# First gate blocks of an expert in front of the branch that picks its body, and shared by all bodies (Trainium2, one core)

## The reference, cut to what matters

```
def moe_swiglu(h, w_router, w_gu, w_down):
    logits = (h @ w_router).astype(jnp.float32)
    top_vals, top_idx = lax.top_k(logits, TOP_K)
    gates = jax.nn.softmax(top_vals, axis=-1)
    comb = ...
    for e in range(N_EXPERTS):
        y = y + comb[..., e:e + 1] * swiglu(h, w_gu[e], w_down[e])
```

## Time and profile before

| | us |
|---|---|
| median of 3 runs | 1783.42 (1782.84 to 1784.57) |
| the profiled execution | 1783.2 |
| its span, first to last instruction | 1781.4 |
| mean granted clock of TensorE, share of full | 0.962 |
| from the first gate matmul of expert 0 to the last of the program | 648 to 1771 |

### The profile page before, as it was taken

How to read it: one execution, slowest core, us unless ns; L and a number is a source line. 1 busy time by engine, 2 the same in 40 slices (tenths; PEclk the granted TensorE clock), 3 DMA queues, 4 the chain that set the end, 5 groups by cost and what they waited for, 6 DMA issues and landing times.

```text
span 1781.4 us, 20893 instructions
## 1 busy us (share of the span) xinstructions
PE 1637.2 (92%) x7345; PEld 1330.9 (75%) x7346; DVE 1267.4 (71%) x1092; ACT 1021.9 (57%) x872; POOL 10.6 (1%) x26
## 2 busy tenths in 40 slices
PE   7999999999899869999999999899999599898996
PEld 5887778888787657777778878778887477677775
DVE  6745554444588569999988888555554599799796
ACT  4344343443456537878867767544443488687684
POOL 0000000000000000000000000000000000000000
PEclk9999999999999869999999999899999799899998
DMA  9653455555522129999999889656564399899894
GB/s 355 194 189 109 163 177 189 188 188 189 188 97 71 47 76 377 397 365 387 394 345 370 329 322 364 237 185 212 192 217 156 126 382 395 296 386 395 302 394 177
DMA packets 191592, 450.84 MB, mean 253 GB/s; under 512 B 8492, under 2 KB 8892, under 8 KB 191420
## 3 DMA queue, kind: packets, MB, share of 16 engines
q1 hardware_dynamic: 189212, 445.35, 69.8%
q10 hardware_dynamic: 2336, 4.85, 0.7%
HBM read 449.13 MB, written 1.05 MB: 253 GB/s over the span
## 4 chain that ended last, share of the span: by engine, by line
PE 71%; DVE 11%; DMA 8%; ACT 5%; issue 4%; DVEq 0%; SPq 0%; ACTq 0%; POOL 0%; POOLq 0%
PE bank L1140 19%; PE bank L1141 19%; PE bank L1144 19%; DMA raw<-in_moe_w_down 8%; DVE wlo L691 6%; PE bank L1147 4%; ACT whi L396 4%; PE bank L1148 3%; DVE y L929 2%; PE bank L1417 1%; PE bank L1418 1%; PE bank L1315 1%; PE bank L1317 1%; PE bank L1433 1%; PE bank L1434 1%
## 5 line engine op out<-in xcount | busy, mean ns | idle before, releaser
L691 DVE TENSOR_TENSOR wlo<-raw,whi 128x2048 fp32r<-128x2048 f32 x422 | 962.6, 2290 | 323.1 <-ACT whi L396 322.2
L396 ACT ACTIVATE whi<-raw 128x2048 fp32r<-128x2048 f32 x422 | 804.9, 1915 | 457.6 <-PE bank L1144 376.9
L1140 PE MATMUL bank<-whi,xx 128*128 128x512 f32 x1184 | 481.3, 406 | 62.7 <-issue 28.1
L1141 PE MATMUL bank<-wlo,xx 128*128 128x512 f32 x1184 | 473.2, 400 | 0.0
L1144 PE MATMUL bank<-whi,xx 128*128 128x512 f32 x1184 | 473.0, 400 | 0.0
L1140 PEld LDWEIGHTS bank<-whi,xx 128*128 128x128 f32 x1184 | 230.2, 194 | 114.5 <-issue 35.9
L1144 PEld LDWEIGHTS bank<-whi,xx 128*128 128x128 f32 x1184 | 229.3, 194 | 49.8
L1141 PEld LDWEIGHTS bank<-wlo,xx 128*128 128x128 f32 x1184 | 230.2, 194 | 46.7
L1147 PE MATMUL bank<-whi,hT 128*128 128x512 f32 x336 | 138.8, 413 | 23.7 <-DVE wlo L691 22.5
L1147 PE MATMUL bank<-whi,xx 128*128 128x512 f32 x336 | 133.3, 397 | 0.2 <-DVE wlo L691 0.2
L1148 PE MATMUL bank<-wlo,hT 128*128 128x512 f32 x336 | 132.3, 394 | 0.0
(11 more groups left out here) (200 smaller groups left out, 1246.0 us busy)
## 6 DMA issues: line engine op xcount, KB each, us to landing
raw<-in_moe_w_gu SPq DMA_DIRECT2D x224, 1024.0 KB, 7.6
raw<-in_moe_w_down SPq DMA_DIRECT2D x112, 1024.0 KB, 7.8
raw<-in_ffn_w_gu SPq DMA_DIRECT2D x28, 1024.0 KB, 5.1
raw<-in_ret_w_in SPq DMA_DIRECT2D x24, 1024.0 KB, 6.6
raw<-in_ffn_w_down SPq DMA_DIRECT2D x14, 1024.0 KB, 4.8
raw<-in_conv_w_pw SPq DMA_DIRECT2D x12, 1024.0 KB, 5.1
raw<-in_ret_w_out SPq DMA_DIRECT2D x8, 1024.0 KB, 4.9
res<-in_x SPq DMA_DIRECT2D x2, 512.0 KB, 4.9
```

What stands on the lines that cost most here:

```text
L396: nc.scalar.activation(whi[base % SPLIT][:, :], raw[base % RAW][:, :], ACT.Copy).then_inc(hi_done, 1)
L691: nc.vector.tensor_tensor(wlo[base % SPLIT][:, :], raw[base % RAW][:, :], whi[base % SPLIT][:, :].bitcast(f32), ALU.subtract).then_inc(lo_ ...
L1140: nc.tensor.matmul(dst, ah, bh, start=start, stop=False)
L1141: last = nc.tensor.matmul(dst, ah, bl, start=False, stop=stop and al is None)
```

## The change

TensorE: tile 0's two gate blocks leave the bodies and are issued once, behind the load of `need` and in front of the branches (`gates_first(0, ...)`), without raising `pe_done`. The bodies stand in the order light to wide. A body begins with `nothing`, a matmul of 4 columns that adds zeros to bank 0; in a narrow body it raises `pe_done` by 2. In a wide body the order is now: `nothing`, gather of tile 1, wait for `yl_done`, scatter, wait for the new semaphore `xel2_done`, tile 1's gate blocks, which raise `pe_done` by 2. ScalarE: `hi` of block 1 is in front of `xh_gathered2`. VectorE: the low part of tile 1 is behind `lo` of block 1 and `y_lo`, and raises `xel2_done`.

```diff
@@ ScalarE, expert @@
                 xh_gathered(e)
+                hi(B_MOE + 1, six)
                 if tiles == 2:
                     xh_gathered2(wide_before(act, e))
-                hi(B_MOE + 1, six)
                 y_hi(B_MOE + 6 * six)
@@ VectorE, expert @@
-                xl_gathered(e, tiles, n2)
+                xl_gathered(e)
                 lo(B_MOE + 1, six)
                 y_lo(e)
+                if tiles == 2:
+                    xl_gathered2(n2)
                 lo(B_MOE + 2, six)
@@ TensorE @@
+            def nothing(dst):
+                return nc.tensor.matmul(dst[:, 0:4], zeros[:, 0:P], zeros[:, 0:4], start=False, stop=True)
...
+            def gates_first(tile, six):
+                for half in range(2):
+                    pe.wait_ge(lo_done, B_MOE + half + 1 + 6 * six)
+                    slot_ = (B_MOE + half) % SPLIT
+                    for c in range(4):
+                        kc = 4 * half + c
+                        last = product(bank[tile][:, :], xh[:, kc, tile, :], xl[:, kc, tile, :],
+                                       whi[slot_][:, c * BANK:(c + 1) * BANK], wlo[slot_][:, c * BANK:(c + 1) * BANK],
+                                       kc == 0, tile == 1 and kc == DC - 1)
+                return last
+
             def expert(e, kinds):
                 six, done, tiles = STEPS * e, STEPS * e + STEPS, len(kinds)
                 gates = (FULL,) * tiles
                 n2 = wide_before(pe, e) if tiles == 2 else None
+                gates_end = nothing(bank[0])
                 if tiles == 2:
                     gather(e, 1).then_inc(gather2_ps, 1)
-                pe.wait_ge(xel_done, e + 1)
-                columns(B_MOE, bank[0:2], 0, kinds=gates, six=six)
-                columns(B_MOE + 1, bank[0:2], 1, kinds=gates, six=six)
-                pe.wait_ge(yl_done, e + 1)
-                scatter(0, SCAT).then_inc(scat_ps, 1)
+                    pe.wait_ge(yl_done, e + 1)
+                    scatter(0, SCAT).then_inc(scat_ps, 1)
+                    pe.wait_ge(xel2_done, n2 + 1)
+                    gates_first(1, six).then_inc(pe_done, 2)
+                else:
+                    gates_end.then_inc(pe_done, 2)
+                    pe.wait_ge(yl_done, e + 1)
+                    scatter(0, SCAT).then_inc(scat_ps, 1)
                 pe.wait_ge(hTl_done, done)
@@ TensorE, loop over the experts @@
                 need = need_of(pe, e)
-                with pe.If(need > 1):
-                    with pe.If(need > 2):
-                        expert(e, (FULL, FULL))
-                    with pe.Else():
-                        expert(e, (FULL, HALF_FULL))
+                pe.wait_ge(xel_done, e + 1)
+                gates_first(0, STEPS * e)
+                with pe.If(need < 1):
+                    expert(e, (HALF_FULL,))
                 with pe.Else():
-                    with pe.If(need > 0):
+                    with pe.If(need < 2):
                         expert(e, (FULL,))
                     with pe.Else():
-                        expert(e, (HALF_FULL,))
+                        with pe.If(need < 3):
+                            expert(e, (FULL, HALF_FULL))
+                        with pe.Else():
+                            expert(e, (FULL, FULL))
```

More of the change, by code:

```diff
@@ L237, in trunk @@
         xel_done = sem("xel_done")
+        xel2_done = sem("xel2_done")
         ohT_ps = sem("ohT_ps")
@@ L1048, in _, with xl_gathered @@
             own(last)
-            def xl_gathered(e, tiles, n):
+            def xl_gathered(e):
                 for q in range(2):
@@ L1054, in xl_gathered, with xl_gathered2 @@
                                                    xh[:, 4 * q:4 * q + 4, 0, :].bitcast(f32), ALU.subtract)
[L1055 to L1060, removed]
-                last.then_inc(xel_done, 1)
+                last.then_inc(xel_done, 1)
+            def xl_gathered2(n):
+                dve.wait_ge(xeh2_done, n + 1)
+                for q in range(2):
+                    last = nc.vector.tensor_tensor(xl[:, 4 * q:4 * q + 4, 1, :],
+                                                   bank[2 + q][:, :].rearrange("p (c n) -> p c n", c=4),
+                                                   xh[:, 4 * q:4 * q + 4, 1, :].bitcast(f32), ALU.subtract)
+                last.then_inc(xel2_done, 1)
             def y_lo(e):
```

## The result

The changed kernel takes 1769.78 us (median, 1765.62 to 1771.41), the kernel before 1783.13 beside it: a ratio of 0.992 with a 95% interval of 0.9904 to 0.9937, so 0.8% faster. The forecast was 1769.2. The profiled execution took 1770.99 us, of which the span is 1769.2; the span before was 1781.4, so the trace has to account for 12.2 us.

The account below looks back on a forecast made before the run. TensorE, busy 92% of the span, was taken to stand idle at expert starts waiting for its own code. Terms -2.5 + 6.6 + 5.6 - 6.1 - 11.0 - 6.6 = -14.0 took 1783.2 to 1769.2 us; own range 1765 to 1773.

Parts of the forecast that it names:

- (a): Start of expert 0: first gate block starts 4.0 earlier, second finds its split done; -2.5 us, between -4 and 0.
- (b): First use of the loop's end in page 22: expert 1 now begins with a stall; +6.6 us, between 0 and 8.2.
- (c): Later weight-slot release delays ScalarE's block 3 split: +1.4 us per HALF_FULL expert, +5.6 for experts 1, 5, 6 and 7.
- nothing makes it up: HALF_FULL steps: VectorE, 14.68 busy of 15.12, bounds them, so the late release's 1.4 us per expert stays.
- (d): Start of wide expert 4: gates fill the 3.89 idle, scatter then waits 3.4 for yl; -6.1 us, between -9 and 0.
- (e): Start of expert 5: one stall of 3.8 to 5.3, first gates at 1390.7 instead of 1401.67; -11.0 us.
- (f): Starts of experts 6 and 7: five pages in use instead of seven, one of two stalls gone; -6.6 us.
- R1: Rival: both later stalls, at experts 6 and 7, go since five pages are few; 1761 us, chance 0.24.
- R3: Rival: far loop end, page 22, fetched anew at every boundary, starts of 1, 2, 3 stall; 1797.5 us, chance 0.08.
- R4: Rival: stalls belong to the loop's way back alone, not the branch into a body; +7.9, 1791 us, chance 0.07.
- R2: Rival: both later stalls stay, since the wide body pushes out page 14; 1776 us, chance 0.15.
- R5: Rival: late release costs its upper bound, +5.2, and the wide start brings half; 1777 us, chance 0.08.

Follow-up runs that it names:

- experiment 4: Changed kernel with ScalarE's y_hi put ahead of the second gathered tile's evacuation in the wide body alone: 1764.27 us, ratio 0.9897.
- experiment 2: Kernel before with only TensorE's four bodies reordered light to wide, first gates left in each body: 1764.94 us, ratio 0.991.
- experiment 3: Changed kernel with its bodies back in the order wide to light, gates still shared ahead of the branches: 1763.68 us, ratio 0.99.
- experiment 11: Changed kernel with y_hi early, slots released one by one, no 4-column matmul, bodies ordered FULL+HALF_FULL, unused FULL+FULL, FULL, HALF_FULL: 1752.91 us, ratio 0.9836.
- experiment 12: Kernel before without the never-run TensorE body for two FULL tiles: 1744.29 us, ratio 0.9791.
- experiment 8: Kernel before with only the release changed: pe_done rises by 2 behind the second first-gate block, not by 1 behind each: 1783.18 us, ratio 1.0008.
- experiment 10: Changed kernel with the first two blocks' weight slots released one by one and the 4-column matmul left out: 1766.46 us, ratio 0.9915.
- experiment 1: Changed kernel without the never-run TensorE body for two FULL tiles: 1757.24 us, ratio 0.9867.
- experiment 7: Changed kernel with last two bodies swapped, y_hi ahead of the second evacuation, slots released one by one, no 4-column matmul: 1754.94 us, ratio 0.9861.
- experiment 6: Changed kernel with only the last two bodies swapped, so FULL+HALF_FULL touches the loop's end: 1764.59 us, ratio 0.99.
- experiment 9: Kernel before, gates left in each body, bodies ordered HALF_FULL, FULL, unused FULL+FULL, FULL+HALF_FULL: 1771.88 us, ratio 0.9942.
- experiment 5: The changed kernel measured again, unaltered, as reference on another chip: 1769.67 us, ratio 0.992.

## Why the prediction was right, and which of its steps were not

The time was right to 0.6 us, the sum of the terms (-14.0) to 1.8. That closeness is luck: five of the six terms were off by 1.2 to 6.8 us, one of 7.6 was missing, and the errors cancelled. What was right is the mechanism and the sign. TensorE waiting for its own code decided the time: taking out code that never runs moved it by 12 and 38 us and changed the packets of the instruction queue with it, and the largest effect of an edit that left the layout of the code alone was the 5 of experiment 4.

(a) Expert 0: -2.5 forecast, -3.7 measured, but for the wrong reason. The step took the wait of 5.99 at its name, a wait for the second block's split, but the first gate waits for the first block's alone, which was done. It said that the branch ran where the gates now run. Experiment 2 has the whole gain without moving a gate, and from 636 to 650 us the instruction queue has four packets in the kernel before and none in the changed one or in experiment 2. What went is the fetch of the far narrow body.

(b) First use of the loop's end: +6.6 forecast, +7.2 measured, a hole of 3.58. Right, and the hole is gone where the loop's end follows the narrow body (experiments 3, 11 and 12).

(c) Late release: +5.6 forecast, nothing measured (experiments 8 and 10). The delay itself was right: ScalarE's split of block 3 waits, the first hidden product comes 1.2 late and the next step's first gate 1.3. But the narrow experts without a hole (1 to 2 and 6 to 7 in the rows above) took 115.6 and 115.7 us where 1.4 more than 115.3 was forecast. The step that failed is "nothing makes it up". It took VectorE's load in a steady step, 14.68 of 15.12, for that of the first step, which has 1.64 us of slack. The hidden product of the next step was not looked up.

(d) Wide start: -6.1 forecast, -4.0 measured. The wait for yl was foreseen to 0.1 us (3.4 against 3.48). But the order alone gains 8 us, 364.80 to 356.80, and the new order of work at the wide start, with y_hi queued late, gave 4 of them back; experiment 4 has them again. The sum did not split the term by part of the change, so it did not see that one part lost.

(e) Start of 5: -11.0 forecast, -4.2 measured. One fetch was assumed where three packets follow on each other; the hole stayed at 14.63, 8.2 above its floor of 6.4. This term was the most wrong, by 6.8.

(f) Starts of 6 and 7: -6.6 forecast for one stall, -13.3 measured for both, 6.65 and 6.64. So it was as R1 had it; its time, 1761, wasn't reached because of (e) and of the hole below. The price of a stall, 6.6 to 8.2 us from the earlier trace rows, held at the starts of 6 and 7 and, as whole stretches, before 1 and 3 (6.6 to 7.6 in the changed kernel, its second trace and experiment 1). It did not hold everywhere: in experiment 4 holes of 3.57 before 1 and 3.15 before 3 made the stretches only 5.0 and 3.7 longer.

Not in the sum: +7.6 before expert 3. It is one of the three places that R3 named; R3 wanted two of the first three starts to stall, and two did (1 and 3), but its mechanism, a fetch of the far end at every boundary, is out: experts 2, 6 and 7 jumped as far without a hole. R4 (the way back alone) is out by experiments 1 and 12, R2 (both later stalls stay) by the trace, R5 by experiment 8. The chances did not quite close: R3 and R4, both slower, had 0.15 together, and slower was given 0.12.

The page from the Trainium skill (Runtime: NRT & Kernel Launch, Instruction fetch mechanics) was weighed rightly. After the wide expert, experiment 7 fetches nothing, though each narrow expert jumps from page 15 to 22 and back to 14; a window of two pages can't do that. Its size of eight pages for TensorE is neither shown nor refuted here. A loop of six pages, 14 to 19 (experiment 1), fetched nothing behind the wide expert, and neither did the nine pages of experiment 7, 14 to 22, of which some never run; one of seven, 14 to 20 (experiment 12), still fetched three behind it, without a hole above the floor.

What stays open is which page is dropped when. Between experiments 6 and 9, with the gates in the bodies and half a page more, the start of 5 got 2.7 us longer and four packets came from 1200 us on instead of one. No run tests whether the oldest page goes or the one longest unused, and the hole before expert 3 is not explained. And the gates' share of experiment 3, where they went ahead of the branch and the code got half a page shorter at once, was not separated.

## What to carry to other kernels

Count the instructions of a loop with branches by pages of 256, the bodies that never run included: taking one of these out was worth 2.1% in the kernel before, more than any rearrangement, and some 0.7% in the changed one. If a body has to stay, try the orders, as experiments 6, 7 and 11 did: the hole before expert 1 was missing wherever the loop's end followed the narrow body. Then read each start in TensorE's timeline for idle time put down to issue, and for waits put down to an engine that had long done its part. And cost each part of a change by itself: two halves that each gave 19 us gave 13 together, because they cured the same holes and their costs lay at different starts.

## What the runs showed of the hardware that was not expected

A hole for code costs more than its length, and not always the same: with holes of 3.1 to 3.6 us the stretches were 3.7 to 7.6 longer. In experiment 4 it was 5.0 before expert 1 and 3.7 before 3, with a granted clock of 0.79 and 0.76 in the gates behind the hole; in experiment 5 it was 6.7 and 6.6, with 0.64 and 0.67. The clock behind the hole isn't all: before expert 3 in experiment 6 it was 1.00, and the stretch was 4.8 longer for a hole of 3.28. The stretches of the first gates of expert 2, without a hole ahead of it, and of expert 3, behind one, in the changed kernel:

```profile
884.07:889.60 5.53, 5.53 (x27) 1.00 1.05 387
1018.07:1026.20 8.13, 8.13 (x24) 0.66 0.69 251
```

Fetches behind each other add up: the hole of 14.63 before expert 5, up to 1403.80, has three packets in it, at 1393.1, 1398.5 and 1398.6 us, while the hole of 3.58 before expert 1 has one, at 762.8, just ahead of its start. And packets need not bring a hole where another wait covers them: in experiment 12 two stand around the start of expert 5, at 1378.2 and 1382.4 us, and its first gates at 1378.99 had waited the 6.4 us for VectorE's xl pair as in experiment 1, which has no packet there.
